# Five elementwise products of the DeltaNet blocks, made by GpSimd in place of VectorE

## The reference

```python
a_mat = where(strict, einsum("nbhid,nbhjd->nbhij", k_beta, k) * decay, 0)
lhs = a_mat + eye
value = triangular_solve(lhs, v * beta)
kcd   = triangular_solve(lhs, k_beta * exp(gc))
qk = einsum("nbhid,nbhjd->nbhij", q, k) * decay
def step(state, ...):
    v_new = value_i - kcd_i @ state
    out = (q_i * exp(gc_i)) @ state + qk_i @ v_new
    k_w = k_i * exp(g_last - gc_i)
    state = state * exp(g_last) + k_w^T @ v_new
```

## Time and profile before

| what | value |
|---|---|
| median of 3 runs | 2016.49 us (2016.30 to 2016.98) |
| the profiled execution's own time | 2016.86 us |
| its span in the trace | 2015.1 us |
| busy PE, DVE, ACT, POOL | 1926.2, 1499.4, 1126.6, 73.7 us |
| mean granted TensorE clock | 0.966 of full |

### The profile page before, as it was taken

How to read it: one execution, slowest core, us unless ns; L and a number is a source line. 1 busy time by engine, 2 the same in 40 slices (tenths; PEclk the granted TensorE clock), 3 DMA queues, 4 the chain that set the end, 5 groups by cost and what they waited for, 6 DMA issues and landing times.

```text
span 2015.1 us, 27100 instructions
## 1 busy us (share of the span) xinstructions
PE 1926.2 (96%) x10976; PEld 1645.9 (82%) x10976; DVE 1499.4 (74%) x1868; ACT 1126.6 (56%) x1249; POOL 73.7 (4%) x67
## 2 busy tenths in 40 slices
PE   9988989889999997988999999999999999999998
PEld 8976868889998986767978888888888888888886
DVE  8657585565547657665588888988889888888986
ACT  5543323333334643423477777777777777777775
POOL 1002011000000001111000000000000000000000
PEclk9997889899999997988999999999999999999999
DMA  7400000545434400002489999999999999999994
GB/s 301 165 27 1 1 1 12 209 148 178 164 121 185 137 27 1 1 1 84 179 320 349 353 354 357 351 341 356 349 360 350 342 355 349 360 352 367 355 360 183
DMA packets 64196, 443.57 MB, mean 220 GB/s; under 512 B 8172, under 2 KB 8204, under 8 KB 13632
## 3 DMA queue, kind: packets, MB, share of 16 engines
q1 hardware_dynamic: 62032, 437.87, 58.2%
q0 software_dynamic: 1760, 3.78, 0.5%
q10 hardware_dynamic: 272, 0.10, 0.0%
HBM read 440.66 MB, written 2.17 MB: 220 GB/s over the span
## 4 chain that ended last, share of the span: by engine, by line
PE 88%; DVE 10%; issue 1%; ACT 0%; DMA 0%; POOL 0%; SPq 0%; DVEq 0%; POOLq 0%; ACTq 0%
PE ps L1891 23%; PE ps L1893 22%; PE ps L1892 22%; PE ps L2278 2%; PE ps L2263 2%; PE ps L2282 2%; PE ps L1904 2%; DVE cacc L1245 2%; DVE w_lo L1153 2%; PE ps L2057 1%; PE ps L2434 1%; PE ps L2445 1%; PE ps L2104 1%; PE ps L2140 1%; PE ps L2069 1%
## 5 line engine op out<-in xcount | busy, mean ns | idle before, releaser
L1210 DVE TENSOR_TENSOR m_lo<-raw,m_hi 128x2048 fp32r<-128x2048 f32 x336 | 768.4, 2290 | 135.8 <-ACT m_hi L810 135.5
L810 ACT ACTIVATE m_hi<-raw 128x2048 fp32r<-128x2048 f32 x336 | 644.1, 1918 | 268.9 <-PE ps L1893 268.9
L1891 PE MATMUL ps<-m_hi,xe_hi 128*128 128x512 f32 x896 | 358.5, 400 | 0.0
L1892 PE MATMUL ps<-m_hi,xe_lo 128*128 128x512 f32 x896 | 353.6, 395 | 0.0
L1893 PE MATMUL ps<-m_lo,xe_hi 128*128 128x512 f32 x896 | 353.6, 395 | 0.0
L1153 DVE TENSOR_TENSOR w_lo<-raw,w_hi 128x1024 fp32r<-128x1024 f32 (+1 forms) x164 | 183.6, 1155 | 126.3 <-ACT w_hi L775 126.3
L1891 PE MATMUL ps<-u_hi,w_hi 128*128 128x272 f32 x800 | 237.0, 296 | 14.7 <-DVE u_lo L1203 10.2
L1893 PE MATMUL ps<-u_lo,w_hi 128*128 128x272 f32 x800 | 233.2, 291 | 0.0
L775 ACT ACTIVATE w_hi<-raw 128x1024 fp32r<-128x1024 f32 (+1 forms) x164 | 159.7, 1002 | 129.9 <-PE ps L1893 124.5
L1892 PE MATMUL ps<-u_hi,w_lo 128*128 128x272 f32 x800 | 232.0, 290 | 0.0
L1893 PEld LDWEIGHTS ps<-m_lo,xe_hi 128*128 128x128 f32 x896 | 168.0, 187 | 41.1
(11 more groups left out here) (397 smaller groups left out, 2766.9 us busy)
## 6 DMA issues: line engine op xcount, KB each, us to landing
raw<-in_moe_units SPq DMA_DIRECT2D x336, 1024.0 KB, 4.9
raw<-in_dense_units SPq DMA_DIRECT2D x57, 1024.0 KB, 4.8
raw<-in_dense_units SPq DMA_DIRECT2D x16, 768.0 KB, 5.0
raw<-in_dense_units SPq DMA_DIRECT2D x8, 896.0 KB, 4.5
w_uq<-in_mla_w_uq SPq DMA_DIRECT2D x2, 768.0 KB, 4.4
mats<-in_c_mats POOLq DMA_DIRECT2D x1, 1216.0 KB, 10.6
h<-in_h_rows SPq DMA_DIRECT2D x2, 544.0 KB, 4.4
bias_rows<-bias_row POOLq DMA_DIRECT2D x1, 1088.0 KB, 26.4
```

The source lines that it names most:

```text
L810: nc.scalar.activation(m_hi[k % RING][:, :], raw[:, slot, :], ACT.Copy).then_inc(m_hi_ready, 1)
L1210: V.tensor_tensor(m_lo[k % RING][:, :], raw[:, mslot(k), :], m_hi[k % RING][:, :].bitcast(F32), ALU.subtract).then_inc(m_lo_ready, 1)
L1891: mm(o, w[0], x[0], start=first, stop=False)
L1892: mm(o, w[1], x[0], start=False, stop=False)
```

## The change

VectorE's list `later` goes, and with it the 40 side products of a run (five for each of two layers, two halves and two directions). GpSimd makes them instead: after the two masks of level `n` (1 to 5) it makes one kind for both directions: `vb` behind level 1's masks, `pt_tri` (q-k under the triangular mask) behind level 2's, `qe` behind level 3's, `pt` (times the decay) behind level 4's, `kw` behind level 5's. The shapes, operands and results of the products are as before. `qe` waits for ACT's `expcols`, `pt` for GpSimd's own `pt_tri`. VectorE waits for `vb` before L1621, PE for `kw` before the output products L2304; the other kinds stand ahead of `kw` in GpSimd's order. DVE's wait for its own `T` ahead of the two products of a level goes too. Nothing else moves.

```diff
+SIDES = ("vb", "pt_tri", "qe", "pt", "kw")
...
 def dn_pool_order():
-    return [("mask", s, n, d) for s in range(2) for n in range(1, LEVELS) for d in range(2)]
+    out = []
+    for s in range(2):
+        for n in range(1, LEVELS):
+            out += [("mask", s, n, d) for d in range(2)]
+            if n <= len(SIDES):
+                out += [(SIDES[n - 1], s, d) for d in range(2)]
+    return out
...
+                        for d in range(2):
+                            if n > len(SIDES):
+                                break
+                            kind, t, c = SIDES[n - 1], (s, 1 - s)[d], 16 * d
+                            x = {k: v[:, :, :] for k, v in batch[d].items()}
+                            tok = slice(META + P * t, META + P * t + P)
+                            if kind == "vb":
+                                out_, in0, in1 = x["Vb"], v_tok[:, t, :, :], bc(gcol[:, t, 1, 4 * d:4 * d + 4], 2, P)
+                            elif kind == "pt_tri":
+                                out_, in0, in1 = x["PT"], qk[:, t, :, :], bc(mat(M_TRI + d), 1, H)
+                            elif kind == "qe":
+                                dn_act.wait(pool, l, "expcols", s, d)
+                                out_, in0, in1 = x["QE"], qkv[:, 0:4, tok], x["QE"]
+                            elif kind == "pt":
+                                dn_pool.wait(pool, l, "pt_tri", s, d)
+                                out_, in0, in1 = x["PT"], x["PT"], x["DT"]
+                            else:
+                                out_, in0, in1 = x["KW"], k_tok[:, t, :, :], bc(cols[:, c + 4:c + 8], 2, P)
+                            dn_pool.mark(nc.gpsimd.tensor_tensor(out_, in0, in1, ALU.mult), kind, s, d)
...
-                    later = []
-                    for d in range(2):
-                        c, t = 16 * d, tiles[d]
-                        later += [(B[d]["Vb"], v_tok[:, t, :, :], bc(bd[d], 2, P)),
-                                  (B[d]["PT"], qk[:, t, :, :], bc(mat(M_TRI + d), 1, H)),
-                                  (B[d]["QE"], qkv[:, 0:4, tok[d]], B[d]["QE"]),
-                                  (B[d]["PT"], B[d]["PT"], B[d]["DT"]),
-                                  (B[d]["KW"], k_tok[:, t, :, :], bc(cols[:, c + 4:c + 8], 2, P))]
...
-                        if later:
-                            own("T", s, n, 1)
-                        for _ in range(min(2, len(later))):
-                            V.tensor_tensor(*later.pop(0), ALU.mult)
...
+                        dn_pool.wait(dve, l, "vb", s, d)
                         link(V.tensor_tensor(B[d]["T"], heads(ps[:, 2 * d, :]), bc(cols[:, c + 12:c + 16], 2, P), ALU.mult))
...
+                        dn_pool.wait(pe, l, "kw", s, d)
                         for hh in range(H):
```

## The result

The changed kernel takes 1989.8 us (median of 4 runs, 1989.48 to 1990.49) against 2016.39 us before; the ratio is 0.9875, with a 95% interval of 0.9856 to 0.9895. Its profiled execution took 1989.56 us, its span is 1987.8 us, and the mean granted clock rose from 0.966 to 0.975.

The account below looks back on a forecast made before the run. PE was taken to bound the kernel (88% of the chain), so DVE's work costs only where PE waits. The sum: 2016.86 - 6.8 - 8.1 - 0.3 + 1.0 = 2002.7 us, called 2002; range 1997 to 2016.

Parts of the forecast that it names:

- Place C: Layer 1, half 0, end of level 0: value wait goes, transposes still wait, low-clock stretch stays; gain 0.3 us.
- A: Layer 0, half 0, end of level 0: 1.09 us wait shrinks to about 0.7, low-clock stretch goes; gain 6.8 us.
- What may be given back: First levels of layer 1: earlier arrival may lengthen low-clock stretches; 1 us lost as mean, 3 us to either side.
- B: Layer 0, half 0, end of level 2: both PE waits and the low-clock stretch behind them go; gain 8.1 us.
- Side products on GpSimd: Forty new GpSimd products at 1.27 us each, 1.72 us as upper end, none below 1.26 us.
- Half 1: Half 1 of both layers: PE never idle in the levels, so taking work from DVE there gains nothing.
- the cases with one or both of them left: Layer 0's two low-clock stretches: only one goes, 2009 us, chance 0.30; neither goes, 2016 us, chance 0.15.
- the slower one: Level 2, half 0: GpSimd's holds delay `T`, PE waits for L1604 or L1607, new low-clock stretch; 2024 us, chance 0.10.

Follow-up runs that it names:

- the second profile: Changed kernel run once more, unaltered: 1992.17 us (6 executions, 1989.57 to 2014.13); the profiled execution took 1989.57 us.
- layer 1 alone: Against the kernel before, GpSimd makes the side products in layer 1 only, VectorE those in layer 0: 2010.6 us, ratio 0.9976.
- half 0 alone: Against the kernel before, GpSimd makes the side products in half 0 of both layers, VectorE those in half 1: 1990.43 us, ratio 0.987.
- layer 0 alone: Against the kernel before, GpSimd makes the side products in layer 0 only, VectorE those in layer 1: 2000.45 us, ratio 0.993.
- the kernel before with fillers from A to C alone: Kernel before plus small ones-matrix products ahead of PE's waits at three places and at layer 0's level 1 end: 2003.24 us, ratio 0.9935.
- the kernel without side products: Against the changed kernel, nobody makes the forty side products; their readers take other operands, so the output differs: 2001.37 us, ratio 0.9918 to the kernel before.
- the runs with fillers: Small ones-matrix products ahead of nearly all PE waits around the mixers: changed kernel 1983.0 us, kernel before 1994.37, version with nobody making side products 1982.8.

## Why the prediction was right and where it failed

**The step that failed** is "Place C": "PE's value products no longer wait, its transposes still do, so the low stretch stays. Gain 0.6 us at the low clock, 0.3 us." In the changed kernel the value products have no wait, as forecast, but the transposes have none either, and the stretch is down to 3.40 us. The gain was mis-sized with it: from `x` of level 0 to the matmul behind `x` of level 2 the trace shows 6.7 us won (the same matmuls start at 768.91 before and 752.33 after, then at 794.63 and 771.35: the lead grows from 16.58 to 23.28 us), the second profile shows 6.7 us too, layer 1 alone measured 5.7 us as a median, and filling C's idle time in the kernel before gave 5.7 us as well. Even where the transposes did wait (1.57 us, with layer 1 or half 0 alone) the stretch was 10.2 us, not 13.65, and C gave 2.5 us, not 0.3. I had priced C by the waits that stay, and given the ones that go no share in the fall. For A I had used the opposite rule: its waits shrink, so the whole stretch goes. C's term makes 6.4 us of the 12.5 us by which the time fell short of the forecast, the next paragraph's some 4 us. The longer wait for the masks at C, which the forecast did not have, isn't GpSimd's new work: with layer 0 alone, where GpSimd makes no side products in layer 1, it is 1.90 us.

**"What may be given back", +1 us,** had the wrong sign: the stretch of 10.24 us at the start of half 1 in layer 1 was gone, and the lead grew by about 3 us there. The idle times ahead of it are the same. The timeline of PE before, then after:

```profile
878.64 0.53 PE L2069 MATMUL ps<-mats,pr 128*96 128x128 f32 x3 [0.25 <-DVE pr L1444]
879.96 0.73 PE L2139 MATMUL ps<-mkn,mqn 128*128 128x272 f32 x2 [0.79 <-ACT ss L954]
...
882.38 1.97 PE L2261 MATMUL ps<-mats,dn_M 128*128 128x128 f32 x8 [1.04 <-DVE dn_M L1576]
```

```profile
854.73 0.53 PE L2084 MATMUL ps<-mats,pr 128*96 128x128 f32 x3 [0.26 <-DVE pr L1470]
856.05 0.72 PE L2154 MATMUL ps<-mkn,mqn 128*128 128x272 f32 x2 [0.78 <-ACT ss L980]
...
858.48 1.26 PE L2276 MATMUL ps<-mats,dn_M 128*128 128x128 f32 x8 [1.05 <-DVE dn_M L1602]
```

The first row that shows the difference is the last of each: 1.97 us and 1.26 us for the same eight matmuls. Both profiles of the changed kernel lack this stretch and the profiles with only one layer or one half moved have it. But the change doesn't decide it. With half 0 alone the code up to there is the changed kernel's (VectorE's first side product of that half starts at 865.10 us), and the eight matmuls take 1.97 us (start 861.00 us). In the kernel before with fillers from A to C alone the code there is unchanged, and they take 1.26 us (start 868.15 us). My 1 us was a mean of stretches that come or don't, and what was measured, 4 us from it, lay outside the 3 us to either side that I had allowed.

**Places A and B** were forecast at 6.8 + 8.1 = 14.9 us and gave 15.6 in the trace, 15.8 with layer 0 alone. B went in each point as predicted: no wait, L1414 and L1415 unhindered (0.15 and 0.50 us), `x` of level 3 not waiting for `T`. A's first wait came to 0.20 us and not 0.7 (0.38 in the second profile), mostly since the `vb` products take 1.08 us. But the sum was right for partly wrong reasons, and part of it was luck. The size of its waits, on which I had hung A's stretch, doesn't decide it: the kernel before's own code passed A without a fall behind 1.22 and 0.50 us, and the kernel without side products fell behind 1.10 and 0.50. That the clock fell at A in none of the four profiles without fillers that have layer 0's side products on GpSimd speaks for the change there, but four profiles don't settle it. And the price of 6.4 us for a stretch, all clock, is not what stands behind it: held at the full clock, the kernel before loses some 8 to 11 us to the changed one in waits, since PE then meets VectorE's side products at the end of level 1 too, a place that I had not seen because the low clock covered it. Clock and waits are two faces of the same idle time, and the profile shows one of them at a time.

**Side products on GpSimd** at 1.27 us: right for `pt_tri`, `qe` and `pt`; `vb` and `kw`, with an operand repeated along the row, took 1.08 and 1.04 us, below the 1.26 that I gave as the lower bound. **Half 1** at nothing: right (1990.43 against 1989.8 to 1992.2 us). **The rivals:** both low stretches of layer 0 went, so the cases with one or both of them left did not come up, and PE never waited for `T` (L1622 or L1625), so the slower one did not either. The Trainium skill's "GPSIMD Engine Reference", section "Engine selection", puts elementwise work on VectorE; GpSimd is slower per product here too (medians of 1.04 to 1.28 us against 0.60), and the move still wins: GpSimd was idle, and its holds cost nothing that the runs with fillers can tell (1982.8 against 1983.0 us).

## What to carry to other kernels

Price work that is taken from an engine at the waits of the engine that bounds the kernel, and look for these waits not only where the trace shows them but also where a PE at 1.2 GHz would meet them if it came at 2.4: a low stretch hides the next wait. Where PE idles in short waits, try a few small products into a free bank first; here they gave 5.7 us at one place without touching any other engine's work, and 7 us on top of the change (1983.0 us, with 1983.55 us the fastest versions that leave no work out). And don't price a low stretch by the clock ratio where PE waits for another engine in it.

## What the hardware showed that I had not expected

- The same waits came with a fall of the clock at one time and without one at another: 1.60 and 0.50 us without, 1.09 and 0.49 or 1.10 and 0.50 us with, and in a single execution 1.22 and 0.50 us without, 1.22 and 0.52 us with. How long a low stretch lasts isn't settled by the idle time in it either: behind the masks of C it was 3.40 us after a wait of 1.88 us in the changed kernel, and 17.10 us after 1.90 us with layer 0 alone, where this stretch is:

```profile
757.40:774.50 17.10, 16.77 (x72) 14.50 (x72) 10.99 (x33) 3.44 (x12) 2.61 (x2) 0.50 0.00 1
```

  What ends it stays open; no run here tells.
- Raising the mean clock from 0.975 to 0.995 with fillers gave 7 us, and in the kernel before from 0.966 to 0.995 it gave 22 us.
- The two kinds of GpSimd products of 128x512 float32 whose second operand repeats one number along the row were 0.2 us shorter than the others (1.04 and 1.08 against 1.27 us).
